# Loading x in two halves and the first weights in six pieces, with more fill products on TensorE, in a two-layer convolution, gMLP and MoE trunk

## The reference

```python
def gated_short_conv(x, w_in, conv_w, w_out):
    b_gate, c_gate, xt = jnp.split(x @ w_in, 3, axis=-1)
    y = b_gate * causal_depthwise_conv(c_gate * xt, conv_w)
    return y @ w_out

for i in range(DEPTH):
    ...
    x = layer_norm(ALPHA * x + h, ln1_g[i], ln1_b[i])
    f = moe(x, router_w[i], router_bias[i], exp_w_gate[i], exp_w_up[i], exp_w_down[i],
            sh_w_gate[i], sh_w_up[i], sh_w_down[i])
    x = layer_norm(ALPHA * x + f, ln2_g[i], ln2_b[i])
```

## Time and profile before

| what | value |
|---|---|
| time, median of 3 runs | 1344.94 us (1344.16 to 1346.04) |
| the profiled execution | 1344.52 us, span 1342.8 us |
| mean granted TensorE clock | 0.965 of full |
| busy share PE, PEld, DVE, ACT, POOL | 91%, 55%, 38%, 24%, 1% |
| mean DMA rate | 349 GB/s |
| chain that ended last | PE 59%, DMA 33% |
| input products of layer 0 (L591) on the chain | 11.57 to 82.41 us |

### The profile page before, as it was taken

How to read it: one execution, slowest core, us unless ns; L and a number is a source line. 1 busy time by engine, 2 the same in 40 slices (tenths; PEclk the granted TensorE clock), 3 DMA queues, 4 the chain that set the end, 5 groups by cost and what they waited for, 6 DMA issues and landing times.

```text
span 1342.8 us, 19213 instructions
## 1 busy us (share of the span) xinstructions
PE 1227.3 (91%) x7592; PEld 737.2 (55%) x7592; DVE 516.6 (38%) x1096; ACT 322.4 (24%) x539; POOL 9.3 (1%) x29
## 2 busy tenths in 40 slices
PE   8999999988888988899999999999998888888998
PEld 8986444444344443348999997644543434344443
DVE  5656333222222222236476666622321222222213
ACT  4442112111111111214544443211111111111110
POOL 0000000000000000000000000000000000000000
PEclk9999999988889989999999999999999888999989
DMA  9956889999999999989544436589999999999993
GB/s 331 393 200 255 332 331 423 420 421 421 421 421 420 422 421 421 420 321 399 188 172 177 163 122 254 208 346 390 421 421 421 420 421 421 420 421 422 421 420 132
DMA packets 83992, 469.10 MB, mean 349 GB/s; under 512 B 7209, under 2 KB 19625, under 8 KB 34875
## 3 DMA queue, kind: packets, MB, share of 16 engines
q1 hardware_dynamic: 82448, 463.50, 85.0%
q10 hardware_dynamic: 1451, 4.33, 0.8%
HBM read 466.76 MB, written 1.05 MB: 348 GB/s over the span
## 4 chain that ended last, share of the span: by engine, by line
PE 59%; DMA 33%; SPq 3%; DVE 3%; issue 2%; ACT 0%; POOL 0%; POOLq 0%; DVEq 0%; ACTq 0%
DMA ring<-in_w_up 32%; PE ps L699 21%; PE ps L591 10%; PE ps L603 6%; PE ps L626 5%; PE ps L723 5%; PE ps L679 3%; PE ps L761 2%; PE ps L737 2%; SPq L409 2%; SPq L429 1%; PE ps L770 1%; PE ps L578 1%; PE ps L667 1%; PE ps L876 1%
## 5 line engine op out<-in xcount | busy, mean ns | idle before, releaser
L699 PE MATMUL ps<-ring,xsT 128*32 128x512 f32 (+1 forms) x2432 | 398.0, 647 | 94.1 <-DMA ring<-in_w_up 94.0
L699 PEld LDWEIGHTS ps<-ring,xsT 128*32 128x32 f32 (+1 forms) x2432 | 126.7, 128 | 359.2 <-issue 358.9
L723 PE MATMUL ps<-ring,hidT 128*32 128x512 f32 (+1 forms) x1216 | 189.7, 596 | 1.0 <-ACT hidT L1032 1.0
L1333 DVE SCALAR_TENSOR_TENSOR sig<-sig,slot_gate,ps 128x256 f32<-128x256 f32 x52 | 25.0, 480 | 424.2 <-ACT sig L1028 424.2
L1158 DVE TENSOR_TENSOR ring_low<-ring,wh 128x1024 fp32r<-128x1024 f32 (+1 forms) x112 | 129.2, 1156 | 103.5 <-ACT wh L972 102.8
L972 ACT CAST wh<-ring 128x1024 fp32r<-128x1024 f32 (+1 forms) x112 | 110.6, 989 | 166.8 <-PE ps L591 69.0
L1028 ACT ACTIVATE sig<-ps 128x256 f32<-128x256 f32 x52 | 20.0, 384 | 477.3 <-PE ps L699 477.3
L1347 DVE TENSOR_TENSOR yl<-ps,yh 128x512 fp32r<-128x512 f32 x104 | 72.0, 692 | 131.3 <-ACT yh L1037 131.3
L591 PE MATMUL ps<-xTh,wh 128*128 128x256 f32 x384 | 109.5, 285 | 3.6 <-DVE ring_low L1158 3.6
L723 PEld LDWEIGHTS ps<-ring,hidT 128*32 128x32 f32 (+1 forms) x1216 | 52.2, 119 | 105.4 <-issue 103.6
L591 PE MATMUL ps<-xTh,ring_low 128*128 128x256 f32 x384 | 109.5, 285 | 0.0
(11 more groups left out here) (202 smaller groups left out, 1263.5 us busy)
## 6 DMA issues: line engine op xcount, KB each, us to landing
ring<-in_w_down SPq DMA_DIRECT2D x128, 1024.0 KB, 25.7
ring<-in_w_gate SPq DMA_DIRECT2D x124, 1024.0 KB, 22.1
ring<-in_w_up SPq DMA_DIRECT2D x124, 1024.0 KB, 25.2
ring<-in_b_w_in SPq DMA_DIRECT2D x8, 3072.0 KB, 16.1
ring<-in_a_w_in SPq DMA_DIRECT2D x12, 1024.0 KB, 12.2
ring<-in_b_w_out SPq DMA_DIRECT2D x4, 3072.0 KB, 10.3
ring<-in_w_gate SPq DMA_DIRECT2D x8, 512.0 KB, 6.4
ring<-in_w_up SPq DMA_DIRECT2D x8, 512.0 KB, 8.4
```

Of the source, the lines that this page charges most:

```text
L699: last = nc.tensor.matmul(ps[first:first + width, p, :], xsT[:, c, p * P + first:p * P + first + width], slot_gu(slot_of(layer, k))[:, c], ...
L723: last = nc.tensor.matmul(ps[first:first + width, 4 + h, :], hidT[:, p, kk * P + first:kk * P + first + width], slot_dn(slot_of(layer, k)) ...
```

## The change

It has four parts. The load of x becomes two loads of half the channels each, with a semaphore of its own; the cast and the subtraction are done by halves, and TensorE waits for the second half in the middle of piece 0, after four of its eight chunks. The three loads of fill 0 (256 columns of one group) become six of 128 columns each: C, X, B of the first 128, then of the second; the cast of each of the first six pieces waits for its own load. The semaphore count of slot 0 no longer includes fill 0. And `keep_clock_up` makes 27 products, not 18.

```diff
--- before.py
+++ after.py
@@ -128,7 +128,7 @@
     for l in range(DEPTH):
         for m, (kind, _) in enumerate(FILLS[l]):
             if FILL_SLOT[l][m] == s and (l, m) <= (layer, n):
-                total += 1 if (l, m) == (0, 0) else FILL_DMAS[kind]
+                total += 0 if (l, m) == (0, 0) else FILL_DMAS[kind]
     return 16 * total
 
 
@@ -300,8 +300,9 @@
         assert place[0] <= nc.sbuf_usable_end
         ps = ctx.enter_context(nc.psum_tensor("ps", [P, 8, HALF], FP32))
 
-        g = sems("g", "xT0 x_in const conv_in rw_in rb_in row_in ws_in gb_in iotas converted stored sh_dn first_c first_x "
+        g = sems("g", "xT0 x_in const conv_in rw_in rb_in row_in ws_in gb_in iotas converted stored sh_dn xT1 first0 first1 first2 first3 first4 first5 "
                       "load0 load1 load2 load3 load4 load5 gu0 gu1 gu2 gu3 gu4 gu5 dn0 dn1 dn2 dn3 dn4 dn5 vstep")
+        first_load = [g[f"first{n}"] for n in range(6)]
         load = [g[f"load{s}"] for s in range(RING)]
         gu_load = [g[f"gu{s}"] for s in range(RING)]
         dn_load = [g[f"dn{s}"] for s in range(RING)]
@@ -375,8 +376,12 @@
 
                     dst = ring[:, s, :].rearrange("p (g c n) -> p g c n", g=3, c=KC)
                     src = a_w_in.rearrange("(p c) (g n) -> p g c n", c=KC, g=3)
-                    for gate, first in ((1, g.first_c), (2, g.first_x), (0, sem)):
-                        sp.dma_start(dst[:, gate], src[:, gate, :, j * 256:(j + 1) * 256]).then_inc(sem if n else first, 16)
+                    for gate in (1, 2, 0) if n else ():
+                        sp.dma_start(dst[:, gate], src[:, gate, :, j * 256:(j + 1) * 256]).then_inc(sem, 16)
+                    for dt in () if n else range(2):
+                        cols = slice(dt * P, (dt + 1) * P)
+                        for m, gate in enumerate((1, 2, 0)):
+                            sp.dma_start(dst[:, gate, :, cols], src[:, gate, :, cols]).then_inc(first_load[3 * dt + m], 16)
                 elif kind == "a_out":
                     tiles = [6, 2][j]
                     dst = ring[:, s, 0:tiles * D].rearrange("p (c n) -> p c n", c=tiles)
@@ -452,7 +457,9 @@
                 wait_fill_used(layer, max(n for n, fill in enumerate(FILLS[layer])
                                           if FILL_SLOT[layer][n] == s and fill[0] != "shared"))
 
-            sp.dma_start(xT_in[:], xT0).then_inc(g.xT0, 16)
+            for half in range(2):
+                chunks = slice(half * KC // 2, (half + 1) * KC // 2)
+                sp.dma_start(xT_in[:, chunks], xT0[:, chunks]).then_inc((g.xT0, g.xT1)[half], 16)
             for layer in range(DEPTH):
                 W, o = L[layer], O[layer]
                 for n, (kind, j) in enumerate(FILLS[layer]):
@@ -587,6 +594,8 @@
                 def columns(dst, wh_n, wl_n):
 
                     for c in range(KC):
+                        if layer == 0 and n == 0 and c == KC // 2:
+                            pe.wait_ge(W.xT_split, 2)
                         for a, b in ((wh_n, xTh), (wh_n, xTl), (wl_n, xTh)):
                             last = nc.tensor.matmul(dst, a[:, c, :], b[:, c, :], start=(c == 0 and b is xTh and a is wh_n),
                                                     stop=(c == KC - 1 and a is wl_n))
@@ -940,7 +949,7 @@
                         last.then_inc(o.products, 1)
 
             pe.wait_ge(g.const, 5)
-            keep_clock_up(7, 18)
+            keep_clock_up(7, 27)
             pe.wait_ge(g.row_in, 16)
             for layer in range(DEPTH):
                 W = L[layer]
@@ -964,8 +973,7 @@
 
                 fill = fill_of(layer, PIECES[layer][n])
                 if layer == 0 and fill == 0:
-                    if n < 3:
-                        act.wait_ge([g.first_c, g.first_x, load[0]][n], 16)
+                    act.wait_ge(first_load[n], 16)
                 elif n == 0 or fill_of(layer, PIECES[layer][n - 1]) != fill:
                     act.wait_ge(load[FILL_SLOT[layer][fill]], fill_ready(layer, fill))
                 w, _, wh_n = piece_weights(layer, n)
@@ -1115,8 +1123,10 @@
 
             act.dma_start(conv_w[:], a_conv_w).then_inc(g.conv_in, 16)
             act.dma_start(row[:], rows.rearrange("r (h n) -> (r h) n", h=2)).then_inc(g.row_in, 16)
-            act.wait_ge(g.xT0, 16)
-            nc.scalar.copy(xTh[:], xT_in[:]).then_inc(A.x0_high, 1)
+            for half in range(2):
+                chunks = slice(half * KC // 2, (half + 1) * KC // 2)
+                act.wait_ge((g.xT0, g.xT1)[half], 16)
+                nc.scalar.copy(xTh[:, chunks], xT_in[:, chunks]).then_inc(A.x0_high, 1)
             for layer in range(DEPTH):
                 W = L[layer]
                 mixer(layer)
@@ -1550,8 +1560,11 @@
             step(nc.vector.tensor_tensor(key_row[0:E, :], tie_row[0:E, :], ident[0:E, 0:E], ALU.mult))
             step(nc.vector.reduce_sum(tie_col[0:E, :], key_row[0:E, :], AX.X))
             dve.wait_ge(g.conv_in, 16)
-            dve.wait_ge(A.x0_high, 1)
-            nc.vector.tensor_tensor(xTl[:], xT_in[:], xTh[:].bitcast(FP32), ALU.subtract).then_inc(L[0].xT_split, 1)
+            for half in range(2):
+                chunks = slice(half * KC // 2, (half + 1) * KC // 2)
+                dve.wait_ge(A.x0_high, half + 1)
+                nc.vector.tensor_tensor(xTl[:, chunks], xT_in[:, chunks], xTh[:, chunks].bitcast(FP32),
+                                        ALU.subtract).then_inc(L[0].xT_split, 1)
             for layer in range(DEPTH):
                 W = L[layer]
                 mixer(layer)
```

## The result

| | before | changed |
|---|---|---|
| median (lowest to highest), 8 runs each | 1344.37 us (1342.25 to 1346.04) | 1350.33 us (1347.97 to 1351.12) |
| profiled execution, its span | 1344.52, 1342.8 us | 1350.25, 1348.5 us |
| first input product | 11.57 us | 11.52 us |
| first product of piece 6 | 30.41 us | 33.42 us |
| first output product of layer 0 | 82.41 us | 87.61 us |

The changed kernel is slower: ratio 1.0042, 95% interval 1.0031 to 1.0053, which is 4 to 7 us.

A forecast was written before the change was run, and what follows sets the result against it. TensorE's input products were taken to bound the kernel from 11.57 us on, with shifts passed on whole. A later piece 6 (+2.8 us) and clock (+1.7) gave +4.5 on 1344.52, 1349.0 us; range 1342 to 1352.

The forecast's parts named there:

- The small pieces: First weights in six 512 KB loads: 290 GB/s, 1.81 us a piece, so fill 0 ends 1.8 us later.
- Start of TensorE: First input product at 10.4 us instead of 11.57, with x in halves and the first piece landing at 7.95.
- The fill products: 27 products before the first input product end at 9.9 us, delay nothing and keep the clock up, saving 1.56 us.
- Fill 1: Three weight loads that begin with piece 6: last one by pace at 25.9 us, loses 4.9, lands at 30.8.
- Waiting at piece 6: Piece 6 starts at 33.2 us instead of 30.41, +2.8 us, after TensorE has stood 5.5 us.
- Clock: Lowered TensorE clock after the idle time before piece 6, taken to cost 1.7 us.
- Whole to the end: Every shift of the input products, seen at 82.41 us, is passed on whole to the kernel's end.
- Sum: 2.8 + 1.7 = +4.5 us on the profiled execution of 1344.52 us, giving 1349.0 us; chance 0.53.
- (a): Rival: fill 1 gets ahead of `X`, landing at 25.6 to 27.4 us; time 1342.2 to 1344.0 us; chance 0.27.
- (b): Rival: half the rate for half the packet, 175 GB/s, piece 6 at 40.5 us, time 1356.4 us; chance 0.05.
- (c): Rival, no change: packets at 349 GB/s and a clock that does not drop, +1.0 us, 1345.5; chance 0.15 with (d).
- (d): Rival: fill products don't keep the clock after 10.4 us; no cost, or 1.6 us back under (a); 0.15 with (c).

The follow-up runs named there:

- the one of 2872.75 us: First profiled execution of the changed kernel with `X`, router weights and bias issued twelve pieces later: 2872.75 us, not in that kernel's ratio of 1.0001.

## Why the prediction held, step by step

- *The small pieces.* 290 GB/s was forecast and 290 measured (13 to 16 us), 1.8 us a piece. By the Trainium skill, "DMA: Bandwidth & Descriptors", "Why small descriptors are slow", three fixed cycles a packet make it, as an estimate from that page, 1.63 us a piece; the trace does not agree.
- *Start of TensorE.* 10.4 forecast, 11.52 measured. The step that failed is x: I let its halves move at the 413 GB/s of long rows. The first was there at 5.41 (4.7 forecast), the second at 6.78 (5.95), VectorE was done at 9.1 (8.5), the first piece at 9.07 (7.95). The halves alone land as late. About half a microsecond of it is scatter: in three more executions with the same start the first piece came at 8.5 to 8.7 and the first product at 10.9 to 11.1; in the one of 2872.75 us it came at 8.98.
- *The fill products.* I had them end at 9.9; they ended at 10.81. The pitch was not wrong, its start was: at 6 to 8 us there are 19 records before and 14 in the changed kernel, where TensorE came up to that pitch only after 7 us. In other executions of the same start the 27 products ended at 9.75 and 9.54, as forecast. The profile gives a granted clock of 1.00 in all these stretches. They delayed nothing and kept the clock, as forecast. What they keep is 1.35 us and not 1.56: six pieces at full clock took 17.5 us in each of the runs that kept it, where I had 6 x 2.88 = 17.3. That what they win is lost in the wait before piece 6 was shown with 18 of them: ratio 1.0034 against 1.0042.
- *Fill 1.* 30.8 forecast, 31.07 measured, and so close in part by luck. The forecast was a pace of 25.9 and 4.9 us lost to `X`; measured from the first piece it was a pace of 27.1 and 4.0 us lost, two errors that cancel. The reading behind the 4.9 was wrong too. I had `X` take 1.5 us from the last load of fill 1 in the kernel before; but that load landed at 25.6, and the first packets of X's queue are in the trace only behind 26.0. None of the 1.5 is X's. Of what fill 1 loses, 1.2 us are there without `X`, and `X` adds 3.3 to 3.4: 27.74 with `X` far away, 31.07, 31.01 and 31.10 with it near. That X's start at 20.43 was 1.2 us later than forecast matters little: in the changed kernel, with 18 fill products and with more of them in the wait it went out at 20.43, 21.39 and 20.02. The mechanism, `X` going ahead of weights that are needed first, stands: moving `X` alone took the loss back.
- *Waiting at piece 6.* +2.8 us forecast, +3.0 measured. Idle time 5.5 us forecast, 4.40 measured, since TensorE had started late.
- *Clock.* 1.7 us forecast, 2.2 measured, and 2.05 when fill products took it away. It was mis-sized by half a microsecond, from rows where the idle time was 3.56 and 5.07 us.
- *Whole to the end.* The span after the first output product was 1260.4 us before, 1260.9 in the changed kernel, and 1259.0 to 1262.9 in the other executions shown here. That holds within 2.5 us.
- *Sum.* +4.5 us forecast, +5.2 at the first output product; 1349.0 us against 1350.25 in the profiled execution and a median of 1350.33. Of the rivals, (a) stands refuted by the landing at 31.07, (b) by 290 GB/s, (c) by the same rate and by the clock, (d) by 1.00 at 13 to 16 us.

Open: the traces show 1.3 us won at the first output product with 27 fill products, with and without `X` later, and the ratios show 0.9999 and 1.0000. A gain of 1.3 us is a ratio of 0.9990; the first interval just reaches it, the second (0.9992 to 1.0009) does not. Part of it may be lost later in the kernel; no run here says where. Whether fill 1 keeps its pace without the instruction load wasn't tried.

## What to carry to other kernels

Ask of an early gain what the next load has in hand: here 2.3 us, and two edits that alone cost at most 0.4 us at the first output product, x in halves and the small pieces, used it up together; the third, the fill products, was neither needed for the loss nor a help against it. A load that nobody needs yet, issued behind the engine's progress, comes earlier when the engine does, and then goes ahead of the one that is needed; moving it was worth as much as the whole loss, and so was giving up the small pieces. Products that keep a clock up belong in the wait that ends last.

## What the runs showed of the hardware

- x as one load of 8 KB per partition was there at 5.95 to 6.25 us in six executions, as two loads of 4 KB per partition at 6.5 to 6.85 in six others, in one of which nothing else had changed. The 413 GB/s of 4 KB rows later on gave no hint of it.
- The queue of `X` began to move some 4 us after its issue: its first packets are in the half microsecond from 24.5 (issued 20.43), 25.0 (21.39), 24.0 (20.02), 23.0 (19.17) and 26.0 (21.98). Three times, with `X` issued 9 to 11 us ahead of the landing, fill 1 then landed 3.3 to 3.4 us later than with `X` far away (31.0 to 31.1 for 27.74). With `X` one piece earlier in the kernel before it was 2.3 (27.60 for 25.34). It lost nothing to `X` in the kernel before, where it had landed when `X` began to move.
- An instruction load of 16 KB took one DMA engine for 1.1 to 1.2 us, and the loads of weights that landed after it were 0.6 to 1.5 us behind their pace, in ten executions, those before it on it; that the one causes the other is argued from the order in time.
- TensorE's clock fell to 0.50 in waits of 4.40 and 3.38 us and cost 2.2 and 2.6 us after them; waits of 1.93 and 1.68 us cost nothing. Waits of 3.56 and 4.49 us before the first product cost 1.3 and 1.2 us (576 input products in 70.84 and 70.70 us, for 69.50 where the clock stayed up). So the cost of a wait did not follow its length.
